# The token mixer of a two-block model queued in another order: pool tiles between q and v tiles, branch gates by tanh, VectorE's parts of conv and norms queued later

## The reference

```python
proj = h @ mix_w_in
xp, q, k, v, z, b_raw, a_raw, g_pool, g_dn = split(proj)
ya = (pool(xp) @ pool_w * pool_scale) @ pool_proj
qkv = silu(causal_depthwise_conv([q, k, v], conv_w))     # width 4, 3 x 8 heads x 128
q, k = l2_normalize(q) * 128 ** -0.5, l2_normalize(k)
o = gated_delta_rule_chunked(q, k, v, g, beta)           # chunks of 64: a unit lower triangular
                                                         # solve in each, then a recurrence
yb = (rms_norm(o, dn_norm_g) * silu(z)) @ dn_proj
merged = sigmoid(g_pool) * ya + sigmoid(g_dn) * yb
x = x + gate * (merged @ mix_w_out)
```

## Time and profile before

| | |
|---|---|
| median of 3 runs | 1982.61 us (1979.6 to 1982.63) |
| the profiled execution | 1979.93 us |
| its span, first to last instruction | 1977.7 us |
| granted TensorE clock, mean | 0.983 |
| PE busy | 1904.1 us (96%) |
| DVE busy, ACT busy | 915.2 us (46%), 814.4 us (41%) |

### The profile page before, as it was taken

How to read it: one execution, slowest core, us unless ns; L and a number is a source line. 1 busy time by engine, 2 the same in 40 slices (tenths; PEclk the granted TensorE clock), 3 DMA queues, 4 the chain that set the end, 5 groups by cost and what they waited for, 6 DMA issues and landing times.

```text
span 1977.7 us, 22206 instructions
## 1 busy us (share of the span) xinstructions
PE 1904.1 (96%) x8899; PEld 1462.3 (74%) x8899; DVE 915.2 (46%) x1644; ACT 814.4 (41%) x1327; POOL 130.6 (7%) x158
## 2 busy tenths in 40 slices
PE   7999999999999899999999988998999999999997
PEld 4666666666788788888876765876787878888886
DVE  4555565655542433333236746366444453333322
ACT  5555555555632322322224752483453342222221
POOL 0101111110001000000100010001000110000000
PEclk9999999999999999999999999998999999999999
DMA  6434333432233223222314212112213323232231
GB/s 209 146 138 143 138 139 139 149 139 86 85 139 97 79 96 101 96 96 88 99 50 154 95 59 71 49 65 59 65 54 106 139 75 96 96 99 96 94 99 61
DMA packets 56685, 201.95 MB, mean 102 GB/s; under 512 B 6638, under 2 KB 7094, under 8 KB 55944
## 3 DMA queue, kind: packets, MB, share of 16 engines
q1 hardware_dynamic: 44616, 158.32, 24.0%
q0 software_dynamic: 11968, 42.21, 6.0%
HBM read 195.23 MB, written 5.28 MB: 101 GB/s over the span
## 4 chain that ended last, share of the span: by engine, by line
PE 84%; DVE 7%; ACT 5%; issue 2%; DMA 1%; POOL 0%; DVEq 0%; SPq 0%; ACTq 0%
PE ps L1022 24%; PE ps L1025 23%; PE ps L1023 23%; PE ps L1073 2%; PE ps L1063 2%; PE ps L1109 2%; PE ps L1097 2%; DVE a L1570 1%; DVE wL L1297 1%; DVE a L1573 1%; PE ps L1085 1%; DVE a L1534 1%; PE ps L1046 1%; ACT wH L1646 1%; DMA wr<-wst 0%
## 5 line engine op out<-in xcount | busy, mean ns | idle before, releaser
L1022 PE MATMUL ps<-hH,wH 128*128 128x512 f32 (+1 forms) x1640 | 686.6, 419 | 21.6 <-DVE hL L1337 12.3
L1025 PE MATMUL ps<-hH,wL 128*128 128x512 f32 (+1 forms) x1640 | 645.8, 394 | 0.6 <-DVE wL L1297 0.6
L1023 PE MATMUL ps<-hL,wH 128*128 128x512 f32 (+1 forms) x1640 | 644.9, 393 | 0.0
L1297 DVE TENSOR_TENSOR wL<-wr,wH 128x1024 fp32r<-128x1024 f32 (+2 forms) x285 | 344.0, 1207 | 489.0 <-ACT wH L1646 488.9
L1646 ACT ACTIVATE wH<-wr 128x1024 fp32r<-128x1024 f32 (+2 forms) x285 | 295.2, 1037 | 272.0 <-PE ps L1025 252.2
L1022 PEld LDWEIGHTS ps<-hH,wH 128*128 128x128 f32 (+1 forms) x1640 | 310.9, 190 | 129.7 <-issue 61.4
L1023 PEld LDWEIGHTS ps<-hL,wH 128*128 128x128 f32 (+1 forms) x1640 | 311.0, 190 | 72.3 <-issue 14.6
L1025 PEld LDWEIGHTS ps<-hH,wL 128*128 128x128 f32 (+1 forms) x1640 | 310.0, 189 | 69.6 <-DVE wL L1297 2.0
L1023 PE MATMUL ps<-gffn,wH 128*128 128x512 f32 x352 | 137.0, 389 | 0.0
L1025 PE MATMUL ps<-gffn,wL 128*128 128x512 f32 x352 | 137.0, 389 | 0.0
L1022 PE MATMUL ps<-gffn,wH 128*128 128x512 f32 x352 | 137.0, 389 | 0.0
(11 more groups left out here) (290 smaller groups left out, 1984.5 us busy)
## 6 DMA issues: line engine op xcount, KB each, us to landing
wr<-wst SPq DMA_DIRECT2D x268, 512.0 KB, 3.5
a<-wfd POOLq DMA_DIRECT2D x54, 512.0 KB, 4.6
xT<-wfd POOLq DMA_DIRECT2D x18, 512.0 KB, 6.9
wr<-wst SPq DMA_DIRECT2D x16, 384.0 KB, 3.0
xT<-xin SPq DMA_DIRECT2D x8, 256.0 KB, 4.6
xT<-xin SPq DMA_DIRECT2D x2, 1024.0 KB, 6.0
xsave<-xT SPq DMA_DIRECT2D x1, 2048.0 KB, 8.0
a<-wfd POOLq DMA_DIRECT2D x8, 256.0 KB, 2.9
```

Of the source, the lines that this page charges most:

```text
L1022: e.matmul(o, hi, xh[k], start=k == 0, stop=False)
L1023: e.matmul(o, hi, xl[k], start=False, stop=False)
L1025: i = e.matmul(o, lo, xh[k], start=False, stop=k == t.nk - 1)
L1297: e.tensor_tensor(dst, x, hi.bitcast(F32), ALU.subtract).then_inc(s[name], 1)
```

## The change

1. In each half two `pool_out` (24 steps) now stand between the q and the v tiles, which end at Q + 88 instead of Q + 64. The fillings behind are shorter by as much. In half 1 four `gd` tiles join the fillings behind `zd`; only 26 steps of them are left after the last recurrence, where one `zd` and three `gd` tiles (32 steps) stood.
2. The gates of both branches are `1 + tanh(g / 2)` instead of `sigmoid(g)`; the missing factor 0.5 goes into the sublayer's gate.
3. VectorE's taps of a conv tile are an event of their own (`conv_taps`), one tick after the end of the tile, so behind the split that is queued at the end; silu and square come at end + 6 instead of end + 5. `v_turn` follows its v tile by 12 ticks (Q + 76 + 8j; before Q + 51 + 8j). VectorE's part of the q and k norms (`l2_end`) is queued 8 ticks after ScalarE's, that of the head norms 9 ticks after.
4. One solve step for each tick, Q + 79 to Q + 108; `sol_back` at Q + 109, inverse from Q + 127, recurrence from Q + 141. Head squares and norms of heads 0 to 3 at Q + 94 and Q + 99 (Q + 104, Q + 112).

```diff
@@ Plan.mixer
+        def gd(c, ring):
+            i, _ = zr.take()
+            d = dict(c=c, i=i, free=z_free[i], gds=sig("gds"))
+            yield from self.steps_of(tile("gd", 5648 + 128 * c, ("gds", d["gds"]), ring, d=d))
...
                 if k == 7:
-                    at(clock[0] + 6, conv_act, a)
+                    at(clock[0] + 2, lambda: add("conv_taps", **d))
+                    at(clock[0] + 7, conv_act, a)
+                    if which == "v":
+                        at(clock[0] + 13, v_turn, h)
...
             add("l2", which=which, items=list(l2s), free=list(half_free))
+            at(clock[0] + 8, lambda: add("l2_end", which=which, items=list(l2s)))
...
             add("head_norms", items=items)
+            at(clock[0] + 9, lambda: add("head_norms_end", items=items))
...
-                at(Q + 51 + 8 * j, v_turn, h)
...
             for k in range(1, 31):
-                at(Q + 79 + (2 * k) // 3, lambda k=k: add("solve", half=half, k=k))
-            at(Q + 100, lambda: add("sol_back", half=half))
+                at(Q + 78 + k, lambda k=k: add("solve", half=half, k=k))
+            at(Q + 109, lambda: add("sol_back", half=half))
             for j, step in enumerate(("t", "p5", "y5", "p6", "y6")):
-                at(Q + 125 + 3 * j, inverse, half, step)
+                at(Q + 127 + 3 * j, inverse, half, step)
             if half == 1:
-                at(Q + 104, head_squares, 0)
-                at(Q + 112, head_norms, 0)
-            for which in ("kqv" if half == 0 else "qv"):
+                fills += [[gd(c, pb), 8, 8] for c in range(4)]
+                at(Q + 94, head_squares, 0)
+                at(Q + 99, head_norms, 0)
+            for which in ("kq" if half == 0 else "q"):
                 for h in hs:
                     for _ in conv(which, h):
                         tick()
-            while clock[0] < Q + 108:
+            fill(24)
+            for h in hs:
+                for _ in conv("v", h):
+                    tick()
+            while clock[0] < Q + 110:
                 fill(1)
...
-            while clock[0] < Q + 139:
+            while clock[0] < Q + 141:
...
-            at(B + 2 + 2 * h if h < 4 else B + 8 + 3 * h, zd_out, h)
+            at(B + 2 + 2 * h if h < 4 else B + 9 + 3 * h, zd_out, h)
...
-        for c in range(3):
-            gd(c)
         while events:
             tick()
         for c in range(8):
             dn(c)
-            if c < 5:
-                gd(c + 3)
+            if c < 4:
+                for _ in gd(c + 4, pb6):
+                    tick()
@@ VectorE
-                        e.tensor_tensor(X[d["c"]], ps[d["bank"]][:], gpb, ALU.mult).then_inc(s["m1"], 1)
-                elif what == "out_conv":
-                    t, d = d["t"], d["d"]
+                        e.scalar_tensor_tensor(X[d["c"]], gpb, 1.0, ps[d["bank"]][:], ALU.add, ALU.mult).then_inc(s["m1"], 1)
+                elif what == "conv_taps":
...
-                    e.tensor_tensor(v, ps[t.bank][:], v, ALU.mult).then_inc(s["dn1"], 1)
+                    e.scalar_tensor_tensor(v, v, 1.0, ps[t.bank][:], ALU.add, ALU.mult).then_inc(s["dn1"], 1)
@@ ScalarE
-                    e.activation(gpb, ps[t.bank][:], ACT.Sigmoid).then_inc(s["gps"], 1)
+                    e.activation(gpb, ps[t.bank][:], ACT.Tanh, scale=0.5).then_inc(s["gps"], 1)
...
-                    e.activation(zb3[d["i"]], ps[t.bank][:], ACT.Sigmoid).then_inc(s["gds"], 1)
+                    e.activation(zb3[d["i"]], ps[t.bank][:], ACT.Tanh, scale=0.5).then_inc(s["gds"], 1)
```

More of the change, by code:

```diff
@@ L494, in zd @@
             yield from self.steps_of(tile("zd", 3584 + 128 * h, ("zds", zds), h=h, zds=zds))
+        zr, z_free, gds = Ring(range(4)), [("i7", 4)] * 4, []
+        def gd(c, ring):
+            i, _ = zr.take()
+            d = dict(c=c, i=i, free=z_free[i], gds=sig("gds"))
+            yield from self.steps_of(tile("gd", 5648 + 128 * c, ("gds", d["gds"]), ring, d=d))
+            self.h_lasts[3] = len(self.slots)
+            gds.append(d)
         fills = [[pool_out(c), 12, 12] for c in range(8)]
@@ L854, in model_kernel @@
         oH, oL = G.several(8), G.several(8)
-        B = Arena(Mb, "b3", 9728)
-        zb3, tq, tr = B.several(3), B.several(8), B.several(8)
+        B = Arena(Mb, "b3", 4096)
+        zb3, tq = B.several(4), B.several(4)
         Mb.close()
-        hb = [P5[:, 0:512], P6[:, 0:512], P6[:, 512:1024], vT[0], tq[4], tq[5], tq[6], tq[7]]
+        hb = [P5[:, 0:512], P6[:, 0:512], P6[:, 512:1024], DT[0]] + tq
         dsol = nc.dram_tensor("dsol", (4 * 65536,), F32, kind="Internal").ap()
@@ L1439, in _ @@
                         e.tensor_tensor(a, a, S("ng", 8 * sub, 8 * sub + 8), ALU.mult)
-                        e.tensor_scalar(gate[:, 8 * sub:8 * sub + 8], mod[:, j + 16:j + 24], 1.0 if sub == 1 else 0.5, None,
+                        e.tensor_scalar(gate[:, 8 * sub:8 * sub + 8], mod[:, j + 16:j + 24], 0.5, None,
                                         ALU.mult, ALU.bypass).then_inc(s["modd"], 1)
@@ L1536, in _ @@
                     e.scalar_tensor_tensor(out, v[:, 1:513], cw(0), out, ALU.mult, ALU.add).then_inc(s["conv"], 1)
-                elif what == "l2":
+                elif what == "l2_end":
                     scale = 1.0 if d["which"] == "k" else 128 ** -0.5
@@ L1617, in _ @@
                                                    ALU.mult, ALU.add).then_inc(s["st"], 1)
-                elif what == "head_norms":
+                elif what == "head_norms_end":
                     for a in d["items"]:
@@ L1890, in _ @@
                     if d["g"] == 0:
-                        w.wait_ge(s["dvt"], DNH)
+                        w.wait_ge(s["pqo"], DNH)
                     for h in range(4 * d["g"], 4 * d["g"] + 4):
```

## The result

| | before | after |
|---|---|---|
| median | 1982.62 us (4 runs, 1979.6 to 1983.33) | 1991.66 us (4 runs, 1991.32 to 1992.47) |
| ratio | | 1.0049, 95% interval 1.0032 to 1.0067 |
| profiled execution, its span | 1979.93, 1977.7 us | 1991.32, 1989.2 us |

The account below looks back on a forecast made before the run. It took TensorE, busy 96% of the span, as the bound, so only its waits and slow clock matter. Terms 9.4 + 4.7 - 4.5 - 5.8 + 3.1 + 3.5 = +10.4 on 1979.93 gave 1990.3, stated as 1991, range 1972 to 2001.

Parts of the forecast that it names:

- The serial chain of a conv tile: Conv tiles: taps behind the low split make one serial loop of 6.8 us a tile, above TensorE's 5.46.
- The delay of the sum: End of the q tiles: TensorE's sum waits for the last square, 8.8 us later in half 0.
- the 1.0 added in each half for half clock: Conv tiles: 1.0 us added to each half's loss because half clock follows long waits.
- Prep, solve, inverse: Prep to the inverse: shorter stretch, gain 4.5 us in half 0 and 5.8 in half 1.
- Recurrence: First update of the recurrence: new wait of about 1.4 us, with half clock 1.7, loss 3.1.
- the one that "falls away": Recurrence of half 0: a like wait two ticks from the new one disappears; half 1 had none.
- The end: After the last recurrence: 26 steps of cover instead of 32, loss 3.5 us, between 0 and 6.
- Tanh: Gates: same passes on both engines, nothing added; about three table switches per half leave prep.
- Faster: Rival: the serial conv chain stays under 5.46 us a tile and does not bind; 1976 us, chance 0.26.
- the conv terms: Conv tiles of both halves: losses of 9.4 us in half 0 and 4.7 in half 1.
- Even: Rival: TensorE's lead swallows half of both conv terms; 1982 to 1985 us, chance 0.15.
- Tables: Rival: tanh isn't in silu's table, so gates cost extra loads, up to 8 us, 1998; chance 0.11.

Follow-up runs that it names:

- experiments 1 and 2: 1: changed kernel with taps back at the tile's end, silu at end + 5, 1976.07 us; 2: kernel before with only taps, silu and square moved, 1989.71 us.
- Experiment 8: Changed kernel with taps back at the tile's end, no pool tiles between q and v, and v_turn at its old ticks: 1983.62 us.
- Experiments 5, 9 and 11: Changed kernel with gate tiles 1 and 2 on the six-bank ring (5), 1992.18 us; norms of heads 4 to 7 at B + 5 (9), 1993.01; both (11), 1993.96.
- experiment 3: Changed kernel with sigmoid gates as before instead of tanh: 1998.4 us, ratio 1.0079 to the kernel before.
- the two edits of the end: Gate tiles 1 and 2 on the six-bank ring and norms of heads 4 to 7 at B + 5, added to the 1972.2 us kernel: 1971.38 us.

## Why the prediction was right, and where it was not

**The serial chain of a conv tile: right, by both numbers.** 6.8 forecast, 6.78 measured, and experiments 1 and 2 show that the place of the taps (with their silu and square) makes it. The delay of the sum was forecast as 8.8 and 4.1. Counted from the first copy of each half it is 8.8 (1131.65 - 1079.43 = 52.2 before, 1138.99 - 1078.01 = 61.0 after) and 4.1 (29.1 and 33.2). What was too large was the 1.0 added in each half for half clock. It came (1125.2 to 1131.6 above), but ahead of the sum, while TensorE followed ScalarE's copies anyway, and cost nothing of its own: no copy there waits for TensorE, and the sum at 1138.99 still waits 0.32 for the square. Another 0.7 of half 0 lies between sum and prep, 8.85 before and 8.13 after; 0.5 of it is a wait of `v_turn` for a silu that moved out of this stretch. The wait also stood elsewhere: in half 0 mostly at the tile's bank (L1030 for L1819, 1.05 and 3.24) and only 0.32 at the sum; in half 1 at the sum, 3.08, as forecast.

**Prep, solve, inverse: right in kind, half 1 by 1.3 too good.** The wait of L1185 (before L1177) for the k norm's product was forecast as 2.5 and is 2.48 (L1549, half 0). GpSimd starts 28.7 after prep (28.0 forecast), the inverse waits for the DMA in both halves (3.15 and 6.33), and the stretch takes 82.27 in both, where 81.9 and 81.0 were forecast: the forecast took 2.4 for the blocks' last landing, as in the earlier trace rows, and it is longer now. The same row of the changed kernel:

```profile
a<-dsol POOLq DMA_DIRECT2D x8, 64.0 KB, 4.2
```

In half 1 the blocks were sent for 1.8 sooner after prep than in half 0 (at 1410.30 against 1223.52, from prep at 1335.66 and 1147.12), and the inverse began no sooner: the longest landing is 5.6. So what was saved ahead of that was lost in the landing. Why it takes longer is not shown. Experiment 8 prices the tiles between q and v at 7.5 without the late taps; the terms here were 4.5 and 5.8.

**Recurrence: the sum 1.1 against 3.1.** The loss in half 1 is 3.5, where the forecast had 3.1 (the new wait, 1.4 forecast and 1.26 measured, and half clock). Half 0 was put at no gain from waits, the new one against the one that "falls away". But TensorE's waits there fell from 4.55 (2.52, 0.27, 1.76) to 2.24 (0.98, 1.26), with 3.4 us of half clock both before and after, and the row shows a gain of 2.4.

**The end: the step that failed, 9.6 against 3.5, beyond its own upper bound of 6.** "The chain is shorter by about 1.5 (a silu tile and a table load leave its front), so the wait is 3.6". The wait in front is 3.41, close to the forecast by luck, because it isn't the `dn` step's: it is gate tile 3 waiting for the bank of gate tile 1, whose tanh stands behind the head norms on ScalarE. And the chain isn't shorter by 1.5 but longer by 3.8. VectorE's norm product and the first `dn` tile's last wait, first before, then after:

```profile
1469.83 2.74 DVE L1622 SCALAR_TENSOR_TENSOR o<-o,sml,b 128x512 f32<-128x512 f32 x4 [3.03 <-ACT b L1901]
...
1487.94 0.50 PE L1022 MATMUL ps<-g,wH 128*128 128x512 f32 x1 [1.03 <-DVE g L1297]
```

```profile
1489.75 2.73 DVE L1629 SCALAR_TENSOR_TENSOR o<-o,sml,b 128x512 f32<-128x512 f32 x4
...
1503.61 0.60 PE L1030 MATMUL ps<-g,wH 128*128 128x512 f32 x1 [1.02 <-DVE g L1305]
```

Counted from the last recurrence product (1456.41 and 1468.26), the norm product starts 8.1 later (13.4 and 21.5) and the last head's step 3.8 later (31.5 and 35.3). ScalarE's part, with the table load and the tanh behind it:

```profile
1485.74 1.28 ACT L1924 ACT_TABLE_LOAD   x1
1487.03 0.60 ACT L1924 ACTIVATE b<-ps 128x512 f32<-128x512 f32 x1
```

The table load didn't leave the chain: with gate tiles as filling, a tanh comes behind the norms, and with it a load of 1.28. VectorE's norm product, which item 3 of the change queues 9 ticks later, now stands behind the low split of one gate tile, and that of the next stands between it and the first head's product. Before, it started as soon as ScalarE's first Exp was there; now it starts 4.6 after the last Exp has ended (1485.20). The forecast gave this delay of `head_norms_end` nothing. Then the `dn` steps wait 1.33 and 1.02 too, with two stretches of half clock, 10.2 us together, where the forecast added 0.9 for the clock.

Experiments 5, 9 and 11 show that neither the bank nor the place of ScalarE's norms sets the end, alone or together: each time the tanh starts 18.8 and the last head's step 35.3 after the recurrence, and the loss stays. That moving VectorE's norm product ahead of the gate tiles' splits, or the fourth gate tile behind the recurrence, would shorten it is argued from the rows and wasn't tried. How the 3.8 divide between the late norm product and the gate tiles is open too.

**Tanh: right.** Nothing lost, and about 6 saved against sigmoid in the same order. The Trainium skill, "ScalarE: Activation LUTs", section "What ACT_TABLE_LOAD costs", adds a drain of 1.38 to each switch; the rows disagree. In the changed kernel the split ends at 1140.28, the load starts at 1140.29 and takes 1.28, and the Ln starts at 1141.59.

**The rivals.** Faster (1976): its condition, copies at 5.46 or less, didn't hold. Experiment 1 makes it hold and gives 1976.07. That this is the rival's own number is partly luck: the conv terms measured 11.3 of the 15.6, where the rival took off 14.1, and the rest came from behind prep. Even: half of the conv terms did not vanish. Tables: see experiment 3.

**Why the total came out so near.** The terms were off by -1.8, -1.0, +0.3, +1.3, -2.0 and +6.1, in all +2.9, so the agreement is better than the steps are, and partly luck: the end, too small by 6.1, and the two gains, too large by 1.6, were offset for the most part by three terms that were too large, by 4.8 together. Another 1.4 is that the changed kernel's profiled execution happened to be early ahead of the mixer. So the profiled time came out 1.0 above its forecast (1991.32 against 1990.3), and the median 0.7 above.

**What was left on the table.** The same change with its taps in place and the norm's product a tick earlier is 1972.2, with the two edits of the end 1971.38 (intervals that overlap): 11 us under the kernel before, 20 under the changed one.

## What to carry to other kernels

When part of a step is queued later on one engine, look at what it now stands behind, and follow the loop through all engines until it closes: here one place in a list made two parallel paths of 4.70 us a tile into one of 6.78, and that cost twice what the rest of the change gave. Such a loop is worth computing first, from five rows of two timelines. When filling is moved ahead of a long chain, ask what its own epilogue does in that chain: here the end of the mixer was left with less cover (26 steps instead of 32), and the gate tiles put a table load and two low splits into the chain there.

## What the runs showed of the hardware that was not expected

- A tanh behind a silu needs no table load and neither does an Exp behind the tanh; a sigmoid in that place needs one of 1.28 us, and the Exp behind it another. Over this kernel that is about 6 us.
- In these rows a table load costs its own 1.28 us and nothing beside it: 1.31 from the end of the split at 1140.28 to the Ln at 1141.59.
- Half clock ahead of a point that another engine sets cost nothing here: the 6.4 us at 0.50 from 1125.2 on left the sum where the copies put it.
- The small DMAs that bring the solve's blocks back took 4.2 us to land in the median, before 2.4, and the slowest 5.6; the inverse waited for them.
